# The merge phase of an encoder step cut into two token groups with a six-bank ring

## The reference

```python
def merge(oa, za, ob, zb, w_out):
    return jnp.concatenate([oa * jax.nn.silu(za), ob * jax.nn.silu(zb)], axis=-1) @ w_out

def finish(x, mix, p, post_g, w_gate, w_ple, ple_g):
    h = x + rms_norm(mix, post_g)
    return h + jax.nn.sigmoid(h @ w_gate) * rms_norm(p @ w_ple, ple_g)
```

## Time and profile before

| | |
|---|---|
| median of 3 runs | 874.99 us |
| the profiled execution, its own time | 871.76 us |
| its span, first to last instruction | 869.9 us |
| mean granted TensorE clock | 0.973 |
| TensorE busy in the span | 92% |
| phase `merge` | 604.66 us to 869.9 us |

### The profile page before, as it was taken

How to read it: one execution, slowest core, us unless ns; L and a number is a source line. 1 busy time by engine, 2 the same in 40 slices (tenths; PEclk the granted TensorE clock), 3 DMA queues, 4 the chain that set the end, 5 groups by cost and what they waited for, 6 DMA issues and landing times. The chain is left out here.

```text
span 869.9 us, 13090 instructions
## 1 busy us (share of the span) xinstructions
PE 798.7 (92%) x5207; PEld 714.3 (82%) x5207; DVE 413.7 (48%) x947; ACT 334.0 (38%) x679; POOL 192.5 (22%) x165
## 2 busy tenths in 40 slices
PE   6999999999978989697678999997999998899998
PEld 6999999999966656565468999897999984498998
DVE  6643231011038889587663222232613438966553
ACT  7321011100016778588674444345411213452111
POOL 0122122122111000153433333222211203812220
PEclk9999999999998999979999999998899999899999
DMA  8142343212011000192026666761611100102301
GB/s 326 49 177 114 103 157 106 76 49 82 0 32 43 2 1 1 43 391 68 1 98 226 239 238 233 266 230 49 272 74 49 49 0 25 49 25 90 117 33 78
DMA packets 35993, 92.58 MB, mean 106 GB/s; under 512 B 4696, under 2 KB 13912, under 8 KB 33752
## 3 DMA queue, kind: packets, MB, share of 16 engines
q1 hardware_dynamic: 33488, 82.23, 26.4%
q10 hardware_dynamic: 2448, 9.57, 2.9%
HBM read 76.13 MB, written 16.58 MB: 107 GB/s over the span
## 5 line engine op out<-in xcount | busy, mean ns | idle before, releaser
L233 PE MATMUL in_acc<-in_x_hi,w_hi 128*128 128x384 f32 x216 | 74.7, 346 | 9.4 <-DVE in_x_lo L427 8.7
L234 PE MATMUL in_acc<-in_x_lo,w_hi 128*128 128x384 f32 x216 | 74.1, 343 | 0.0
L235 PE MATMUL in_acc<-in_x_hi,w_lo 128*128 128x384 f32 x216 | 74.0, 343 | 0.0
L233 PE MATMUL in_acc<-in_x_hi,in_w_hi 128*128 128x384 f32 x216 | 72.6, 336 | 0.0
L233 PE MATMUL mrg_acc<-mrg_a_hi,w_hi 128*128 128x384 f32 x192 | 67.0, 349 | 6.1 <-issue 3.0
L235 PE MATMUL in_acc<-in_x_hi,in_w_lo 128*128 128x384 f32 x216 | 72.2, 334 | 0.0
L234 PE MATMUL in_acc<-in_x_lo,in_w_hi 128*128 128x384 f32 x216 | 72.2, 334 | 0.0
L234 PE MATMUL mrg_acc<-mrg_a_lo,w_hi 128*128 128x384 f32 x192 | 65.5, 341 | 0.0
L235 PE MATMUL mrg_acc<-mrg_a_hi,w_lo 128*128 128x384 f32 x192 | 65.4, 341 | 0.0
L233 PE MATMUL mrg_acc<-mrg_a_hi,mrg_w_hi 128*128 128x384 f32 x192 | 64.2, 334 | 0.0
L235 PE MATMUL mrg_acc<-mrg_a_hi,mrg_w_lo 128*128 128x384 f32 x192 | 64.1, 334 | 0.0
(11 more groups left out here) (250 smaller groups left out, 1987.3 us busy)
## 6 DMA issues: line engine op xcount, KB each, us to landing
ahead_ring<-kb_cache SPq DMA_DIRECT2D x16, 1024.0 KB, 7.2
ahead_ring<-vb_cache SPq DMA_DIRECT2D x16, 1024.0 KB, 8.8
qo<-xT SPq DMA_DIRECT2D x16, 576.0 KB, 7.9
w_raw<-w_in SPq DMA_DIRECT2D x11, 512.0 KB, 4.1
plane<-w_in SPq DMA_DIRECT2D x9, 512.0 KB, 3.5
h_scratch<-qo SPq DMA_DIRECT2D x8, 576.0 KB, 5.2
plane<-h_scratch SPq DMA_DIRECT2D x8, 576.0 KB, 15.2
yT<-mrg_mix SPq DMA_DIRECT2D x7, 576.0 KB, 3.1
```

What stands on the lines that cost most here:

```text
L233: pe.matmul(out, w_hi, x_hi, start=start, stop=False)
L234: pe.matmul(out, w_hi, x_lo, start=False, stop=False)
L235: return pe.matmul(out, w_lo, x_hi, start=False, stop=stop)
```

## The change

The phase is cut in two groups of token columns: A is runs 0 and 1 (768 columns, `COLS[0]`), B is run 2 (384). A unit is one run of one block: `UNITS` lists (0,0), (0,1), (1,0), ... (7,1) and then (0,2) ... (7,2), 24 in all (`NU`; the first 16 are `NA`). TensorE does the output projection for A, then for B, then the embedding's 24 units, then the gate for A, then for B. A weight block is loaded and split once for A and once for B: q = 0 to 31 in place of 16 splits. `acc` is a ring of six banks, one for a unit. The embedding's weights have tiles of their own (the tile that held z, once z is used, and a new one). The norms are made for each group apart, in parts between the units; x is loaded for each group apart. Evacuations, squares and sums are of 384 columns, the steps on h of 768 (A) or 384 (B). The decode tokens' norm moves from ahead of the first product to between A's units. The queues, cut to their core (`mix_square(u)` waits for `evacuate(u)`; `ple_square` for `take_ple`; `piece(t, u)` is unit u's part of t):

```diff
-            multiply(0, (a_hi_done, a_lo_done), {1: spread_sub})
-            for j in range(1, NB):
-                multiply(j)
@@ TensorE
+            for u in range(NU):
+                multiply(u, 0, mix_parts)
+                if u == 2:
...
+                    last.then_inc(sub_summed, 1)
+                if u == 5:
...
+                if u == NA:
+                    pe.wait_ge(sub_scaled, 1)
+                    statistics(0, 0)
+                if u == NA + 2:
+                    to_all(0, 0)
+            pe.wait_ge(p_in, 48)
+            for u in range(NU):
+                embed(u)
+                if u == 3:
+                    statistics(0, 1)
+                if u == 6:
+                    to_all(0, 1)
+                if u == 20:
+                    statistics(1, 0)
+            for u in range(NU):
+                multiply(u, 2 * NU, gate_parts)
+                if u == 0:
+                    to_all(1, 0)
+                    statistics(1, 1)
+                if u == 2:
+                    to_all(1, 1)
+            def statistics(which, g):
+                pe.wait_ge(added, NU * which + (NU if g else NA))
+                wait(pe, rms_done, spreads_before(which, g))
@@ ScalarE
+            def high(q):
+                act.wait_ge(w_in[q % 2], 16 * ((q + 1) // 2))
+                if q >= 2:
+                    act.wait_ge(product, last_product(q - 2))
+            def square(u, counted):
+                slot = (counted + u) % 3
+                if counted + u >= 3:
+                    act.wait_ge(added, counted + u - 2)
+            def take_ple(u):
+                wait_h(act, UNITS[u][0], group_of(u))
+                act.wait_ge(product, NU + u + 1)
+            a_high(0)
+            high(1)
+            a_high(1)
...
+            for u in range(NA):
+                mix_square(u)
+                if u == 3:
                     sub_norm.scalar(act)
+                if u == 9:
+                    a_high(2)
+                if u % 2:
+                    high(u // 2 + 2)
+            mix_square(NA)
+            high(NB + 2)
+            norm[0].scalar(act)
+            for u in range(NA + 1, NA + 3):
+                mix_square(u)
+                high(u - NA + NB + 2)
             for j in range(NB):
+                h_high(j, 0)
+                if j % 2:
+                    u = NA + 3 + j // 2
+                    mix_square(u)
+                    high(u - NA + NB + 2)
+            mix_square(NU - 1)
+            high(2 * NB + 1)
+            for u in range(NU):
+                take_ple(u)
+                ple_square(u)
...
+            for u in range(NU):
+                if u == 1:
+                    norm[1].scalar(act, 1)
+                gate(u)
+                q = 2 * NB + use_of(u) + 2
+                if (u >= NA or u % 2) and q < 4 * NB:
+                    high(q)
@@ GpSimd; add(0, 0) and add(2, 0) are VectorE's
+            for q in range(1, NB + 5):
+                low(q)
+            for j in range(NB):
+                add(j, 0)
+                if j % 2:
+                    low(NB + 5 + j // 2)
+            low(2 * NB + 1)
+            for j in range(NB):
+                add(j, 1)
@@ VectorE
+            evacuate(NA)
+            add(NA - 1, 0)
+            mean(0, 0)
+            evacuate(NA + 1)
+            add(NA, 0)
+            invert(0, 0)
+            evacuate(NA + 2)
+            add(NA + 1, 0)
+            keep_rms(0, 0)
             for j in range(NB):
+                scale_mix(j, 0)
+                if j >= 2:
+                    h_low(j - 2, 0)
+                if j % 2:
+                    evacuate(NA + 3 + j // 2)
+                    add(NA + 2 + j // 2, 0)
+            evacuate(NU - 1)
+            add(NU - 2, 0)
+            h_low(NB - 2, 0)
+            h_low(NB - 1, 0)
+            add(NU - 1, 0)
+            mean(0, 1)
+            invert(0, 1)
+            for u in range(5):
+                add(u, NU)
+            keep_rms(0, 1)
             for j in range(NB):
+                scale_mix(j, 1)
+                add(5 + j, NU)
                 if j >= 3:
+                    h_low(j - 3, 1)
@@ SyncE
+            load_weight(4)
+            for half in range(2):
+                if half == 0:
+                    sp.wait_ge(gated, 2)
+                sp.dma_start(ple_half[half][:].rearrange("p (b c) -> p b c", b=4),
+                             w_ple[4 * half:4 * half + 4].rearrange("b p k c -> p b (k c)")).then_inc(p_in, 16)
+            for q in range(5, 2 * NB + 3):
+                load_weight(q)
```

More of the change, by code:

```diff
@@ L1611, in _ @@
+            for q in range(4 * NB - 6, 4 * NB):
+                store_y(q)
+            sp.wait_ge(y_out, 16 * 2 * NB)
         @block.scalar
         def _(act):
[L1613 to L1623, removed]
@@ L1626, in _ @@
[L1626 to L1631, removed]
-                    sub_norm.scalar(act)
-                if k == AG - 1:
-                    high(1)
-            for j in range(2, NB):
-                high(j)
-                act.wait_ge(mix_out, j - 1)
-                square(j - 2, 0)
@@ L1751, in to_all @@
-            def to_all(which):
-                for n in range(NCH):
-                    pe.wait_ge(diag_done, TT * which + TT // NCH * (n + 1))
-                    if n == 2:
-                        pe.wait_ge(rms_done, NCH * which + 1)
-                    pe.matmul(small[:, n % 2, 0:RUN], ones, run(total[:], n), start=True, stop=True).then_inc(spread, 1)
-            def spread_sub():
-                pe.wait_ge(sub_diag, BH)
-                pe.matmul(small[:, 1, :], ones, total[:, 0:BH * P], start=True, stop=True).then_inc(sub_spread, 1)
@@ L1762, in _ @@
-            pe.wait_ge(sub_squared, 1)
-            for h in range(BH):
-                last = pe.matmul(small[:, 0, h:h + 1], work[0][:, h * P:(h + 1) * P], ones[:, 0:1],
-                                 start=True, stop=True)
-            last.then_inc(sub_summed, 1)
-            multiply(0, (a_hi_done, a_lo_done), {1: spread_sub})
-            for j in range(1, NB):
-                multiply(j)
-            pe.wait_ge(p_in, 16)
-            embed(PLE0)
-            statistics(0)
-            embed(PLE0 + 1)
@@ new lines, in statistics, with to_all @@
+            def statistics(which, g):
+                pe.wait_ge(added, NU * which + (NU if g else NA))
+                wait(pe, rms_done, spreads_before(which, g))
+                first = TILES[0] if g else 0
+                for t in range(TILES[g]):
+                    last = pe.matmul(small[:, 0, t:t + 1], total[:, (first + t) * P:(first + t + 1) * P], ones[:, 0:1],
+                                     start=True, stop=True)
+                last.then_inc(sums, 1)
+            def to_all(which, g):
+                for i, n in enumerate(RUNS[g]):
+                    pe.wait_ge(diag_done, diags_before(which, g) + NCH * (i + 1))
+                    pe.matmul(small[:, (1 + i) % 2, 0:RUN], ones, run(total[:], n), start=True, stop=True).then_inc(spread, 1)
@@ new lines, in mean, with invert @@
+            def mean(which, g):
+                dve.wait_ge(sums, 2 * which + g + 1)
+                norm[g].mean(dve, small[:, 0, 0:TILES[g]])
+            def invert(which, g):
+                norm[g].invert(dve, which)
+                first = TILES[0] if g else 0
+                for t in range(TILES[g]):
+                    dve.tensor_scalar(total[:, (first + t) * P:(first + t + 1) * P], ident, norm[g].out[:, t:t + 1], None,
+                                      ALU.mult).then_inc(diag_done, 1)
```

445 lines of the change are left out of this document (222 added, 223 removed).

## The result

The changed kernel takes 894.97 us, the median of four runs (894.15 to 896.46), where the kernel before took 874.51 beside it (four runs, 871.65 to 878.85): a ratio of 1.0234, with a 95% interval of 1.0206 to 1.0262. It is slower, by 20.5 us where 14.0 were forecast; the time lies in the range (873 to 900) and 6 us above the point. The profiled execution took 894.15 us with a span of 892.4, 22.5 more than the span before.

A forecast was written before the change was run, and what follows sets the result against it. TensorE, busy 92% of the span, was taken as the bound. Gains of 14.3 us against 28.3 added, mostly late weight splits, gave net +14.0: 889 us against the median of 874.99, range 873 to 900.

The forecast's parts named there:

- the sign that the size would be wrong: In the profile after: half clock coming back oftener than after the named waits for weights would make the size wrong.
- Start: Phase start: first product near 605.8, no longer waiting for the decode norm, -3.05 us; half-clock loss stays 2.8.
- Weight 5: Output projection for A: load 5 queued behind w_ple loads, unit 10 waits +4.1 us, half clock then +1.7.
- the half clock: TensorE's lower clock after idle times: +1.7 us after weight 5's wait, +2.5 for unit 23 and the first embeddings.
- Out B: Output projection for B: weights 13, 14, 15 split late, units 21 to 23 wait 5.1, 4.3, 5.2, together +14.6 us.
- the turn-taking: SBUF port lock: two-SBUF-input VectorE operations and GpSimd operations alternate whole; without it the +14.6 us would be about +9.
- the splits' place in the lists: GpSimd's and ScalarE's lists: splits of weights 13 to 15 stand behind steps on h, making them some 9 us apart.
- Embedding: Embedding stage: waits of +1.9 us ahead of statistics(0, 1) and +0.8 ahead of statistics(1, 0); bounds 0 and 9.
- Gate: Gate stage: +0.8 us waiting for copies of the factor, +0.6 for splits in B; no wait for h at its start.
- the clock falls with the waits: Rival for B's output projection and the embedding: more half clock, +4 to +12 us, 893 to 901; chance 0.15.
- TensorE stays fed: Rival: B's splits come within 4.2 us and load 5 in time, 864 us; chance 0.12 for all fed.
- no lock: Rival: no lock at 768 columns, B's output-projection waits 9.0 in place of 14.6, 883 us; less-wait case 0.20.

The follow-up runs named there:

- e5_psum: Changed kernel with VectorE's scalings of group A reading the norm's factor from PSUM, in two 384-column pieces, not from its SBUF copy: 894.12 us, ratio 1.0225.
- e4_warm: Changed kernel plus matmuls that compute nothing needed, placed in TensorE's waits ahead of units 10, 21 to 23 and the embedding's statistics: 890.10 us, ratio 1.0181.
- b3_dve_adds: Kernel before with all eight additions of h on VectorE (BY_DVE 0 to 7 in place of 0 and 2): 868.19 us, ratio 0.9936.
- e1_load5: Changed kernel with the load of weight 5 moved ahead of the two w_ple loads in SyncE's list: 887.34 us, ratio 1.0170.
- e6_all: Changed kernel with load 5 early, splits 13 to 15 earlier, group A's additions on VectorE and its scalings reading PSUM: 884.25 us, ratio 1.0120.
- b1_start: Kernel before with only the change's start: output blocks 0 and 1 run by run, decode norm between them: 873.27 us, ratio 0.9987.

## Why the prediction was right, and where its size was off

The sign and the mechanism were right: the gains of the two groups were spent on splits that come too late, with a unit of 4.16 us and no longer a block of 12.48 to hide them. The signs that were named came: the first product at 605.63, the load of weight 5 issued at 647.17 behind those of `w_ple`, `low(13)` to `low(15)` ended 8.7 and 9.4 us apart, scalings of 2.6 and 3.1 us beside GpSimd, and no wait for h at the gate. So did the sign that the size would be wrong: half clock also behind the two `statistics` of the embedding. The span came 8.5 us above the forecast one; between the medians, which are the better measure, the loss is 20.5 where 14.0 were forecast. Step by step, in the profiled execution:

- *Start.* Forecast 605.8, measured 605.63. The clock was not at half there in this execution, but a wait of 2.00 for the second run's `a_hi` at 612.03, which the sum did not have, took the place of that 2.8. Two errors nearly cancel here, by luck.
- *Weight 5.* Forecast ready at 656.1, measured 656.44, behind the list order named. The wait was 4.95 (4.1) and the half clock cost (662.0 - 656.44)/2 = 2.8 (1.7). Unit 16 began at 684.04, 1.2 later than the forecast's own 682.8.
- *Out B.* From unit 16 `low` of weights 13, 14 and 15 ended at 30.7, 39.4 and 48.9 us; forecast 30.2, 38.9 and 48.4. By these arrivals the forecast's own waits would be 5.3 + 4.5 + 5.3, some 0.5 more than the 5.1 + 4.3 + 5.2 that the sum took. In the trace 4.79 + 1.91 + 5.00 = 11.7 were idle; the rest was unit 21 at half clock, some 2.6, which hides in the wait behind it. The stage ended at 55.1 (54.6). That the turn-taking would set it is shown by the rows; that the splits' place in the lists was its cause is half right, since with the place mended most of the same time stood ahead of `statistics(0, 1)`.
- *Embedding.* Here the sum failed by most: the gate began 98.1 us after unit 16 and not 93.1, 4.5 of it in this stage. The waits were 2.48 + 1.65 = 4.1 where 2.7 were taken. The half clock behind each wait cost 1.7 and 3.4, where the sum had none; the units, `statistics` and `to_all` themselves took some 2 us less than the sum had. That this half clock is not hidden the other runs show: from `statistics(0, 1)` to `statistics(1, 0)` are 26.85 us here and 25.16 in `e5_psum`, which has no half clock there, with the same wait of 1.65 at the end; from `statistics(1, 0)` to `statistics(1, 1)` are 15.04 here, 13.4 in the runs with a stretch of 3.4, and 11.69 in `e4_warm`, which has none.
- *Gate.* 2.2 more than forecast, of which the wait of 1.06 at 799.12 is a part; the wait for h was gone, as said.

The term that was mis-sized is the half clock: 1.7 + 2.5 = 4.2 in the sum, and 2.8 + 2.1 (unit 23, from 732.95 to 737.1) + 1.7 + 3.4 = 10.0 in the trace. That is 5.8 of the 8.5, the largest part. In the profiled executions of all five other variants without filling matmuls the last stretch lasted 3.4 us and not 6.8, so 1.7 of the 10.0 belong to this execution. The rival *the clock falls with the waits* joined the forecast: its 893 to 901 holds the result, though with the waits as forecast. `e4_warm`, with most of the half clock taken away behind the same waits, is 4.9 us faster. *TensorE stays fed* and *no lock* are refuted by the waits, and the latter by the scalings of 3.10 and by `b3_dve_adds` too. That weight 5's place was 7.6 us of the loss is shown by `e1_load5`.

What the forecast said of the kernel before has one flaw: of the 8.5 us that it calls idle in the embedding, the trace has 7.9 as idle time, and the clock was at half from 737.4 to 740.8 as well, which is missing in its list of places.

The phase can also be added up as a whole, from its first instruction to the end of the span: idle time of TensorE behind the first product, and half of the time that it worked at half clock, which is an estimate of what that clock cost.

| | phase | to first product | idle | half clock | all the rest |
|---|---|---|---|---|---|
| kernel before | 265.3 | 4.2 | 9.7 | 6.0 | 245.4 |
| changed kernel | 288.0 | 1.3 | 26.1 | 12.5 | 248.1 |
| `e6_all` | 275.9 | 1.3 | 16.6 | 10.8 | 247.2 |
| `b3_dve_adds` | 260.2 | 3.5 | 6.5 | 4.8 | 245.3 |

So of the 10.6 us by which `e6_all` is longer than the kernel before, 7.0 are idle time, 4.7 half clock and 1.8 the rest, and the start gives back 2.9. The one wait of 10.44 ahead of `statistics(0, 1)` is more than all of that idle time, and the half clock behind it costs 2.8. What would remove that wait was not tried.

## What to carry to other kernels

Before cutting a stage in groups, lay out what must be made between two uses of a double buffer against the new, shorter use: here 3.9 us of splitting fitted 12.48 with room to spare, and 4.16 only where nothing stood between the splits. When two engines take turns, count the stretch at nearly both lists together (here some 25 us of each in 45.8): an order that hid a wait mostly moved it. Giving the slower engine's part to the faster one (`BY_DVE`) was the one edit that clearly made the kernel before faster; in the changed kernel its gain of 2.2 us in the stretch did not show in the time. Count a wait of the matmul engine at more than its length where the clock falls with it.

## What the runs showed of the hardware

- An operation with a single tensor input, from SBUF to SBUF, can stand as well: in the changed kernel six scalings of `ident` by a factor (128 columns each) took 3.44 us at 696.91, where GpSimd's `low` ran from 697.49, and 1.27 at 777.60 with GpSimd idle. Nor must the operation be large: one of 3 columns, which reads the same SBUF tile as both inputs, took 2.16 at 795.80, where GpSimd's `low` ran from 795.45, and 0.16 at 748.71 with GpSimd idle. With one operand in PSUM the two scalings of `e5_psum` that met GpSimd were not longer (1.13).
- GpSimd can be the one to stand. In `b1_start` its `low` took 6.55 us in place of 2.40 while eight subtractions of VectorE's followed one another without a gap; none of them was delayed (0.48 us each from start to start):

```profile
611.49 6.55 POOL L1695 TENSOR_TENSOR mrg_w_lo<-mrg_w_raw,mrg_w_hi 128x1024 fp32r<-128x1024 f32 x1 [5.45 <-ACT mrg_w_hi L1617]
```

```profile
611.96 3.83 DVE L1817 TENSOR_TENSOR mrg_a_lo<-qo,mrg_a_hi 128x384 fp32r<-128x384 f32 x8
```

- The clock's state is not fixed by the kernel alone: the start of the phase was at half clock in the profiled execution of before and of `e4_warm`, and not in that of the changed kernel. One execution's clock is a sample.
